# Turning the finished attention output after the next scores instead of before them, with one row-maximum unit moved to the following slot

## What is computed

```python
def mla_attention(q_nope, q_rope, k_nope, k_rope, v):
    scale = (MLA_D_NOPE + MLA_D_ROPE) ** -0.5
    def block(args):
        qn, qr = args
        s = (jnp.einsum('bqhd,bkhd->bhqk', qn, k_nope)
             + jnp.einsum('bqhd,bkd->bhqk', qr, k_rope)).astype(jnp.float32) * scale
        p = jax.nn.softmax(s, axis=-1).astype(v.dtype)
        return jnp.einsum('bhqk,bkhd->bqhd', p, v)
```

## Time and profile before

| what | us |
|---|---|
| median of 3 runs (3678.96 to 3681.22) | 3680.98 |
| the profiled execution, its own time | 3676.88 |
| its span, first to last instruction | 3675.1 |
| PE busy over the span (PEld 2957.8) | 3467.4 |
| DVE, ACT, POOL busy over the span | 2239.5, 1590.4, 831.6 |

### The profile page before, as it was taken

One profiled execution on the slowest core, in us unless ns is written; L12 is line 12 of the kernel. 1 busy time (PEld: TensorE's weight loads), 2 busy tenths in 40 slices (PEclk: granted clock), 3 DMA queues, 4 the chain that ended last, 5 costly groups with the idle time before them and its releaser, 6 DMA issues. The chain is left out here.

```text
span 3675.1 us, 51638 instructions
## 1 busy us (share of the span) xinstructions
PE 3467.4 (94%) x19042; PEld 2957.8 (80%) x19042; DVE 2239.5 (61%) x3925; ACT 1590.4 (43%) x2038; POOL 831.6 (23%) x412
## 2 busy tenths in 40 slices
PE   8999979997999999999799859999999999999996
PEld 6888868885777777777577649999999999999996
DVE  5444457776888888886455465555555555555568
ACT  2111134443676777767332223333333333333466
POOL 0000000003676767767011101111111111111101
PEclk9999989997999999999899869999999999999998
DMA  3111145656133332210433335555555555555676
GB/s 119 62 63 62 64 163 196 214 197 184 32 56 58 57 57 40 50 32 7 158 131 133 116 99 167 167 166 165 167 164 166 167 165 166 165 167 163 194 256 211
DMA packets 342352, 474.65 MB, mean 129 GB/s; under 512 B 105648, under 2 KB 241584, under 8 KB 339536
## 3 DMA queue, kind: packets, MB, share of 16 engines
q1 hardware_dynamic: 329344, 427.10, 37.1%
q0 software_dynamic: 12880, 45.88, 5.6%
HBM read 355.54 MB, written 117.39 MB: 129 GB/s over the span
## 5 line engine op out<-in xcount | busy, mean ns | idle before, releaser
L63 PE MATMUL psum<-xeT_hi,w_hi 128*128 128x320 f32 x2048 | 634.4, 310 | 0.0
L65 PE MATMUL psum<-xeT_hi,w_lo 128*128 128x320 f32 x2048 | 632.8, 309 | 0.0
L64 PE MATMUL psum<-xeT_lo,w_hi 128*128 128x320 f32 x2048 | 632.8, 309 | 0.0
L1357 POOL TENSOR_TENSOR added<-added,p_hi 128x1024 f32<-128x1024 f32 x192 | 458.8, 2389 | 157.4 <-ACT p_hi L1311 156.5
L2267 DVE TENSOR_TENSOR w_lo<-w_raw,w_hi 128x2048 fp32r<-128x2048 f32 x190 | 427.5, 2284 | 30.7 <-ACT w_hi L2102 30.7
L2102 ACT ACTIVATE w_hi<-w_raw 128x2048 fp32r<-128x2048 f32 x192 | 358.4, 1908 | 187.1 <-PE psum L65 187.1
L1393 DVE TENSOR_TENSOR p_lo<-psum,p_hi 128x1024 fp32r<-128x1024 f32 x272 | 332.5, 1222 | 89.4 <-ACT psum L1313 88.4
L63 PEld LDWEIGHTS psum<-xeT_hi,w_hi 128*128 128x128 f32 x2048 | 384.4, 188 | 0.9
L64 PEld LDWEIGHTS psum<-xeT_lo,w_hi 128*128 128x128 f32 x2048 | 384.4, 188 | 0.6
L65 PEld LDWEIGHTS psum<-xeT_hi,w_lo 128*128 128x128 f32 x2048 | 384.4, 188 | 0.0
L1311 ACT ACTIVATE p_hi<-psum 128x1024 fp32r<-128x1024 f32 x272 | 279.3, 1027 | 218.4 <-PE psum L65 218.3
(11 more groups left out here) (364 smaller groups left out, 7165.5 us busy)
## 6 DMA issues: line engine op xcount, KB each, us to landing
w_raw<-in_w_gate SPq DMA_DIRECT2D x64, 1024.0 KB, 5.2
w_raw<-in_w_up SPq DMA_DIRECT2D x64, 1024.0 KB, 7.4
w_raw<-in_w_down SPq DMA_DIRECT2D x64, 1024.0 KB, 5.4
rec<-rec SPq DMA_DIRECT2D x20, 768.0 KB, 3.6
recb<-rec SPq DMA_DIRECT2D x20, 768.0 KB, 5.0
xa<-in_x SPq DMA_DIRECT2D x20, 512.0 KB, 4.5
xb<-in_x SPq DMA_DIRECT2D x20, 512.0 KB, 5.8
v_lo_hi<-v SPq DMA_DIRECT2D x16, 640.0 KB, 9.6
```

Source lines behind the costliest of these rows:

```text
L63: pe.matmul(out, a[0], b[0], start=first, stop=False)
L64: pe.matmul(out, a[0], b[1], start=False, stop=False)
L65: return pe.matmul(out, a[1], b[0], start=False, stop=last)
L1357: g.tensor_tensor(acc[:], so_far, p_hi[at % 4][:].bitcast(F32), ALU.add).then_inc(s["p_added"], 1)
```

## The change

In a turn slot PE now issues the scores first, then the turn, then the mix; the unit of that slot is issued at the head of the next slot, ahead of its scores. ACT does the exponentials before the half copy. DVE makes the low part before it takes the output, and the postponed unit's reduction comes at the head of the next slot's list. No instruction is added or dropped, and no wait is changed.

```diff
                 for g in range(-AHEAD, TOTAL + 3):
+                    if g - 1 in turn_slot and g - 1 + AHEAD < TOTAL:
+                        unit(g - 1 + AHEAD)
+                    if 0 <= g + LATE < TOTAL:
+                        score(g + LATE)
                     if g in turn_slot:
                         turn_out(turn_slot[g], min(g + AHEAD, TOTAL))
-                    if 0 <= g + LATE < TOTAL:
-                        score(g + LATE)
-                    if g + AHEAD < TOTAL and g not in turn_slot:
+                    elif g + AHEAD < TOTAL:
                         unit(g + AHEAD)
                     if 0 <= g < TOTAL:
                         mix(g)
-                    if g + AHEAD < TOTAL and g in turn_slot:
-                        unit(g + AHEAD)
...
                         take_out(last_of.index(g - 1))
+                    if 0 <= g + LATE < TOTAL:
+                        exponentials(g + LATE)
                     if g in turn_slot:
                         take_half(turn_slot[g])
-                    if 0 <= g + LATE < TOTAL:
-                        exponentials(g + LATE)
...
                 for g in range(-AHEAD, TOTAL + 3):
-                    if g in turn_slot:
-                        take_out(turn_slot[g])
-                    if g + AHEAD < TOTAL:
+                    if g - 1 in turn_slot and g - 1 + AHEAD < TOTAL:
+                        reduce(g - 1 + AHEAD)
+                    if g + AHEAD < TOTAL and g not in turn_slot:
                         reduce(g + AHEAD)
                     if 0 <= g + LATE < TOTAL:
                         make_lo(g + LATE)
+                    if g in turn_slot:
+                        take_out(turn_slot[g])
```

## The result

| kernel | median us (lowest to highest) | ratio to before, 95% interval |
|---|---|---|
| before | 3680.02 (3678.96 to 3681.22) | |
| after | 3790.4 (3787.55 to 3793.52) | 1.0299 (1.0283 to 1.0316) |

The sign was right, the size was not: 110 us more where 78 were forecast, and 2 us above the range. The profiled execution took 3787.55 us, its span 3785.8.

What follows compares the result with a forecast made beforehand. The prediction took PE, busy 94% of the span, as the bound. From 3676.88 us, +56 for PE stalls at block ends and +22 for 15 clock falls gave 3755, expected as a 3759 us median, range 3728 to 3788.

Steps and rivals of the forecast that it cites:

- The sign: Whole kernel: the change makes it slower, chance 0.90, against 0.04 for the same and 0.06 for faster.
- the size: Whole kernel: 56 us more from PE's stall at block ends and 22 us more from clock falls, median 3759 us.
- the range: Whole kernel's median: 3728 to 3788 us, from slightly below the stall alone up to 28 clock falls instead of 15.

## What to carry to other kernels

When two engines hand a buffer back and forth, lay out both lists: moving a step behind other work on one engine is only free if the work that answers it is not moved behind something later on the other. A wait of 0.4 us is to be covered with about as much work, not with a whole stage. And an idle time on TensorE that recurs has to be priced twice when it is as long as here (1.85 us): here the stall itself cost 54 us and the lower clock behind it 56 more.

## What the runs showed of the hardware

- Idle stretches of 1.85 us, 37 of them, were followed by a fall of TensorE's granted clock from 1.00 to 0.50 in 35 cases, for about 3.4 us, in seven for twice that. Of 37 stretches each, 3.4 us came with a fall in all 37, 1.65 us in 14, 1.0 us in 6, 0.92 us in none. Eight useless matmuls in each gap gave back 56 us, and four did too. The runs differ in what PE did before the gap as well as in its length (four matmuls more before the 0.92 us; a unit and six score matmuls before the 1.65 us), and which of the two decides was not tried.
- A DVE instruction with two SBUF inputs (0.425 us) took 2.49 us when it started 0.17 us behind the start of a GpSimd add of 2.4 us, and a copy of four columns from SBUF to SBUF took 1.80 us within one, where a reduction over the same four took 0.157. One more wait on GpSimd, which kept the two apart, made a kernel 86 us faster.
